# Attention stage of a two-model kernel: four units in flight, row and column halves of the array in turns, group outputs in one bank

## Reference

```python
R = H // G                                   # 16 heads, 4 groups of keys and values, 64 wide
sc = where(vis, einsum('bgrqd,bgnd->bgrqn', qb, k_cmp), NEG)         # 15 compressed blocks
p_cmp = softmax(sc) * any(vis)
o_cmp = einsum('bgrqn,bgnd->bgrqd', p_cmp, v_cmp)
sc = where(pos <= t, einsum('bgrqd,bgqkd->bgrqk', qb, ksel), NEG)    # selected blocks
o_slc = einsum('bgrqk,bgqkd->bgrqd', softmax(sc), vsel)
sc = where(wmask, einsum('bgrqd,bgkd->bgrqk', qb, kwin), NEG)        # window
o_win = einsum('bgrqk,bgkd->bgrqd', softmax(sc), vwin)
return gb[..., 0:1] * o_cmp + gb[..., 1:2] * o_slc + gb[..., 2:3] * o_win
```

## Time and profile before

| | us |
|---|---|
| median of three runs | 1864.11 |
| lowest and highest run | 1857.58, 1868.36 |
| the profiled execution | 1860.6 |
| its span in the trace | 1858.7 |
| PE busy, of the span | 1715.8 |
| DVE busy | 1038.0 |
| ACT busy | 791.7 |

### The profile page before, as it was taken

The page is one execution under the profiler, slowest core; times in us unless marked ns, Lnnn a source line. Parts: engine busy times, 40 slices in busy tenths (PEclk is TensorE's granted clock), DMA queues, the critical chain, the costliest instruction groups (busy, mean ns, idle before and its releaser), DMA issues.

```text
span 1858.7 us, 22342 instructions
## 1 busy us (share of the span) xinstructions
PE 1715.8 (92%) x8605; PEld 1414.5 (76%) x8605; DVE 1038.0 (56%) x1326; ACT 791.7 (43%) x963; POOL 96.7 (5%) x143
## 2 busy tenths in 40 slices
PE   6999978899999999989898989999899887789996
PEld 6788867688888788889855777888688673668885
DVE  4577654466655676645554435555548653655553
ACT  4434433365434444333455335555444433334441
POOL 1000000010000000010000003000100010200000
PEclk8999989999999999999899999999899895799998
DMA  8687734177864677633400425556365330536550
GB/s 288 201 277 262 233 108 157 40 255 252 268 226 147 229 259 262 225 104 101 167 33 1 139 69 174 190 189 213 108 231 204 109 106 1 170 125 203 181 181 23
DMA packets 210195, 311.74 MB, mean 168 GB/s; under 512 B 16537, under 2 KB 145589, under 8 KB 209872
## 3 DMA queue, kind: packets, MB, share of 16 engines
q1 hardware_dynamic: 204112, 288.90, 46.6%
q0 software_dynamic: 6016, 21.94, 3.4%
HBM read 306.59 MB, written 4.21 MB: 167 GB/s over the span
## 4 chain that ended last, share of the span: by engine, by line
PE 85%; DVE 6%; ACT 3%; issue 3%; DMA 1%; PEld 1%; POOL 1%; DVEq 0%; PEldq 0%; ACTq 0%; SPq 0%; POOLq 0%
PE ps L1994 24%; PE ps L1996 24%; PE ps L1995 24%; DVE wlo L1304 1%; PE ps L2035 1%; PE ps L2330 1%; PE ps L2116 1%; PE ps L2217 1%; PE ps L2315 1%; DMA area<-in_gate_b 1%; PE ps L2045 1%; PE ps L2198 1%; PE ps L2418 1%; PE ps L2306 1%; ACT xn L811 0%
## 5 line engine op out<-in xcount | busy, mean ns | idle before, releaser
L1304 DVE TENSOR_TENSOR wlo<-raw,whi 128x2048 fp32r<-128x2048 f32 x255 | 581.0, 2298 | 238.1 <-ACT whi L757 237.3
L757 ACT ACTIVATE whi<-raw 128x2048 fp32r<-128x2048 f32 x255 | 481.2, 1910 | 207.1 <-PE ps L1996 183.7
L1994 PE MATMUL ps<-wlo,aT_hi 128*128 128x512 f32 (+1 forms) x1280 | 500.2, 391 | 22.1 <-DVE aT_lo L1330 9.2
L1996 PE MATMUL ps<-whi,aT_hi 128*128 128x512 f32 (+1 forms) x1280 | 493.4, 385 | 0.0
L1995 PE MATMUL ps<-whi,aT_lo 128*128 128x512 f32 (+1 forms) x1280 | 493.0, 385 | 0.0
L1994 PEld LDWEIGHTS ps<-wlo,aT_hi 128*128 128x128 f32 x1280 | 244.1, 191 | 72.6 <-issue 15.0
L1996 PEld LDWEIGHTS ps<-whi,aT_hi 128*128 128x128 f32 x1280 | 243.5, 190 | 47.9
L1995 PEld LDWEIGHTS ps<-whi,aT_lo 128*128 128x128 f32 x1280 | 244.2, 191 | 45.1
L1994 PE MATMUL ps<-wlo,hT_hi 128*128 128x512 f32 x480 | 188.0, 392 | 5.4 <-DVE hT_lo L1421 3.0
L1996 PE MATMUL ps<-whi,hT_hi 128*128 128x512 f32 x480 | 187.6, 391 | 0.0
L1995 PE MATMUL ps<-whi,hT_lo 128*128 128x512 f32 x480 | 187.3, 390 | 0.0
(11 more groups left out here) (302 smaller groups left out, 1388.4 us busy)
## 6 DMA issues: line engine op xcount, KB each, us to landing
raw<-in_ffn_w_in SPq DMA_DIRECT2D x176, 512.0 KB, 4.9
raw<-in_ffn_w_out SPq DMA_DIRECT2D x88, 512.0 KB, 4.3
raw<-in_w_ff SPq DMA_DIRECT2D x64, 512.0 KB, 4.7
raw<-in_ada_w SPq DMA_DIRECT2D x48, 512.0 KB, 5.5
raw<-in_w_in SPq DMA_DIRECT2D x48, 512.0 KB, 4.7
raw<-in_xattn_w_kv SPq DMA_DIRECT2D x32, 512.0 KB, 7.0
raw<-in_xattn_w_q SPq DMA_DIRECT2D x16, 512.0 KB, 4.8
raw<-in_xattn_w_o SPq DMA_DIRECT2D x16, 512.0 KB, 4.9
```

The lines of the kernel that those rows point to most:

```text
L757: act.activation(to, of, ACT.Copy).then_inc(hi_ready[slot], 1)
L1304: dve.tensor_tensor(lo, of, hi, ALU.subtract).then_inc(lo_ready[slot], 1)
L1994: pe.matmul(o, lh, rl, start=start, stop=False, skip_group_check=True)
L1996: return pe.matmul(o, lh, rh, start=False, stop=stop, skip_group_check=True)
```

## The change

Nothing is computed that was not computed before, except one exponential of a single column. What moves:

- **Four in flight.** `Pb` gets a fourth buffer and scores a fourth bank (`u % 4`). `nmx`, `den` and `rec` become eight columns wide. What lay in the way moves to `spare`, an unused half of `gain`. DVE and ACT run `top(u + 3)` and `exps(u + 3)` behind `weigh(u)` and `keep(u)`.
- **Rows in turns.** `score_pair(p)` writes the scores of units `2p` and `2p + 1`, lower rows, upper rows, lower rows, upper rows. PE's loop goes over pairs: `score_pair(p + 2)`, `turn(2p)`, `turn(2p + 1)`, then `turn_cmp` or all of `values`.
- **Columns in turns.** `values(gi)` alternates between output partitions 0 to 63 and 64 to 127 term by term, and all groups use bank 7. So `values(gi)` waits for `out_lo(gi - 1)`, where it waited for `out_lo(gi - 2)`.
- **`out_lo` a unit later** in DVE's queue (`u % 4 == 2`).
- **The start.** `score_pair(0)` is issued ahead of the compressed scores, `top(0)` and `top(1)` ahead of the centring, `exps(0)` and `exps(1)` ahead of the compressed branch's exponential, and its weighing moves into the loop behind `weigh(1)` and `top(4)`. ACT issues an exponential of one column first, which loads its table. 20 matmuls of zeros stand ahead of the loop instead of 30; neither loop has any in it.

```diff
-        Pb = [xnf[:, 512 * b:512 * b + 512] for b in range(3)]
+        Pb = [xnf[:, 512 * b:512 * b + 512] for b in range(4)]
+        nmx4, den4, rec4 = small[:, 26:34], small[:, 34:42], small[:, 42:50]
+        spare = gain[:, 1, :]
...
+                    act.activation(small[:, 62:63], minus_half[:, 0:1], ACT.Exp)
+                    exps(0)
+                    exps(1)
                     act.wait_ge(cmp_centred, 1)
                     act.activation(cmpP, cmpP, ACT.Exp).then_inc(cmp_exped, 1)
-                    exps(0)
-                    exps(1)
+                    exps(2)
                     for u in range(32):
                         keep(u)
-                        if u + 2 < 32:
-                            exps(u + 2)
+                        if u + 3 < 32:
+                            exps(u + 3)
...
-                        if u >= 3:
-                            dve.wait_ge(probs_turned, U - 2)
+                        if u >= 4:
+                            dve.wait_ge(probs_turned, U - 3)
...
                     top(0)
                     top(1)
+                    centre_cmp()
+                    top(2)
                     for u in range(32):
                         weigh(u)
-                        if u + 2 < 32:
-                            top(u + 2)
-                        if u % 4 == 1 and u > 4:
+                        if u + 3 < 32:
+                            top(u + 3)
+                        if u == 1:
+                            weigh_cmp()
+                        if u % 4 == 2 and u > 4:
                             out_lo(u // 4 - 1)
...
+                    def score_pair(p):
+                        g, t, k = p // 4, p // 2 % 2, p % 2
+                        w = P * (t + 1)
+                        if p >= 2:
+                            pe.wait_ge(maxed, units.n + 2 * p - 2)
+                        for c, keys in ((0, ksT), (w, kwT)):
+                            for e in range(2):
+                                half = slice(64 * e, 64 * e + 64)
+                                last = pe.matmul(ps[:, (2 * p + e) % 4, c:c + w], qT[half, 2 * g + k, t * P:(t + 1) * P],
+                                                 keys[half, g, 0:w], start=True, stop=True)
+                                if c:
+                                    last.then_inc(scored, 1)
...
-                    def values(gi, half):
+                    def values(gi):
...
-                        if gi >= 2:
-                            pe.wait_ge(o_kept, groups.n + gi - 1)
+                        if gi:
+                            pe.wait_ge(o_kept, groups.n + gi)
+                        terms = [(vcmp[:, 64 * g:64 * g + 64], nsaPc[gi % 2][0:N_CMP])]
                         for j, v in enumerate((vs, vw)):
                             for m in range(t + 1):
                                 c = P * (j * (t + 1) + m)
+                                terms.append((v[:, m, 64 * g:64 * g + 64], nsaP[gi % 2][:, :, c:c + P]))
+                        for n, (v, probs) in enumerate(terms):
+                            for half in range(2):
+                                last = pe.matmul(ps[64 * half:64 * half + 64, 7, 0:256], v, probs[:, half::2, :],
+                                                 start=n == 0, stop=n == len(terms) - 1, skip_group_check=True)
+                        last.then_inc(pv_done, 1)
...
-                    score(0)
-                    score(1)
-                    keep_clock(30, 5)
-                    for u in range(32):
-                        if u + 2 < 32:
-                            score(u + 2)
-                        turn(u)
-                        if u % 4 == 2:
-                            turn_cmp(u // 4)
-                        if u % 4 < 2 and u >= 4:
-                            values(u // 4 - 1, u % 4)
-                    for half in range(2):
-                        values(7, half)
+                    score_pair(1)
+                    keep_clock(20, 4)
+                    for p in range(16):
+                        if p + 2 < 16:
+                            score_pair(p + 2)
+                        turn(2 * p)
+                        turn(2 * p + 1)
+                        if p % 2:
+                            turn_cmp(p // 2)
+                        elif p:
+                            values(p // 2 - 1)
+                    values(7)
```

More of the change, by code:

```diff
@@ L1023, in exps @@
                     def exps(u):
-                        U, t, b = units.n + u, u // 4 % 2, 2 * (u % 3)
+                        U, t, b = units.n + u, u // 4 % 2, 2 * (u % 4)
                         w = P * (t + 1)
@@ L1665, in nsa_attend @@
-                    every = [P, T, NSA_H, N_CMP]
[L1666 to L1671, removed]
@@ L1672, in nsa_attend, with centre_cmp @@
-                    dve.tensor_tensor(cmpP, cmpP, cmp_max.unsqueeze(3).to_broadcast(every), ALU.subtract).then_inc(cmp_centred, 1)
+                    def centre_cmp():
+                        mask = cst[:, C_CMP:C_CMP + 32].rearrange("p (t n) -> p t n", t=T)[:, :, 0:N_CMP]
+                        dve.wait_ge(cmp_scored, 2)
+                        for par in range(2):
+                            scores = ps[:, 6 + par, 0:256].rearrange("p (t h n) -> p t h n", t=T, h=NSA_H // 2)[:, :, :, 0:N_CMP]
+                            step(dve.tensor_tensor(cmpP[:, :, par::2, :], scores,
+                                                   mask.unsqueeze(2).to_broadcast([P, T, NSA_H // 2, N_CMP]), ALU.add))
+                        step(dve.tensor_reduce(cmp_max, cmpP, AX.X, ALU.max))
+                        dve.tensor_tensor(cmpP, cmpP, cmp_max.unsqueeze(3).to_broadcast(every), ALU.subtract)\
+                            .then_inc(cmp_centred, 1)
@@ new lines, in weigh_cmp @@
+                    def weigh_cmp():
+                        dve.wait_ge(cmp_exped, 1)
+                        step(dve.tensor_reduce(cmp_rec, cmpP, AX.X, ALU.add))
+                        step(dve.reciprocal(cmp_rec, cmp_rec))
+                        step(dve.tensor_tensor(cmp_rec, cmp_rec, gates[:, :, 0::3], ALU.mult))
+                        dve.tensor_tensor(cmpP, cmpP, cmp_rec.unsqueeze(3).to_broadcast(every), ALU.mult).then_inc(cmp_weighed, 1)
+                    every = [P, T, NSA_H, N_CMP]
@@ L2298, in nsa_attend @@
                     enter()
[L2300 to L2306, removed]
-                        pe.matmul(ps[:, u % 3, w:2 * w], q, kwT[half, g, 0:w], start=True, stop=True).then_inc(scored, 1)
+                    def score_pair(p):
[10 more added lines that the diff above has]
+                                    last.then_inc(scored, 1)
                     def turn(u):
@@ L2314, in turn @@
                         for m in range(2 * (t + 1)):
-                            last = pe.transpose(ps[:, 3 + u % 2, P * m:P * m + P], Pb[u % 3][:, P * m:P * m + P], ident)
+                            last = pe.transpose(ps[:, 4 + u % 2, P * m:P * m + P], Pb[u % 4][:, P * m:P * m + P], ident)
                         last.then_inc(probs_turned, 1)
-                    def values(gi, half):
+                    def values(gi):
                         g, t = gi // 2, gi % 2
@@ L2329, in values @@
                                 c = P * (j * (t + 1) + m)
-                                last = pe.matmul(o, v[:, m, 64 * g:64 * g + 64], nsaP[gi % 2][:, half::2, c:c + P],
-                                                 start=False, stop=j == 1 and m == t)
-                        if half == 1:
-                            last.then_inc(pv_done, 1)
+                                terms.append((v[:, m, 64 * g:64 * g + 64], nsaP[gi % 2][:, :, c:c + P]))
[4 more added lines that the diff above has]
+                        last.then_inc(pv_done, 1)
                     def turn_cmp(gi):
@@ L2340, in turn_cmp @@
                         for r in range(4):
-                            last = pe.transpose(ps[0:N_CMP, 5, P * r:P * r + P], cmpP[:, t, 4 * g + r, :], ident)
+                            last = pe.transpose(ps[0:N_CMP, 6, P * r:P * r + P], cmpP[:, t, 4 * g + r, :], ident)
                         last.then_inc(cmp_turned, 1)
+                    score_pair(0)
                     for t in range(T):
```

40 lines of the change are left out of this document (16 added, 24 removed).

## The result

| | before | after |
|---|---|---|
| median, us | 1863.88 (4 runs) | 1834.1 (4 runs, 1830.64 to 1836.34) |
| ratio | | 0.984, 95% interval 0.981 to 0.987 |
| span of the profiled execution | 1858.7 | 1830.7 |
| from the end of the matmuls ahead of the stage to its last `out_lo` | 108.4 | 78.1 |
| period of eight units | 21.90 | 14.07 |

What follows compares the result with a forecast made beforehand. PE was taken to bound the attention loop. After: 4 x 14.1 + 1.9 + 3.25 = 61.6 us, ending 31.7 earlier; less 6.0 for the clock, a 25.7 gain takes 1860.6 to 1834.9, range 1822 to 1850.

Steps and rivals of the forecast that it cites:

- What bounds the kernel, PE's blocks: Attention loop: PE bounds it; array halves overlap, so PE's work per period falls by 7.4 to 12.2 us.
- The next bound: Attention loop: ACT's 12.5 us per period is the floor, handovers come above; period 13.3 to 16.0, taken as 14.1.
- The fewer change-overs: PE's loop: fewer changes between block shapes, as a second turn follows a first; not counted, only on the good side.
- `values` waits for the group before: PE's queue stands behind out_lo of the group before; counted as nothing, 1.5 us per group if DVE were late.
- The start: Ahead of the loop: ten fewer zero matmuls at about 0.22 us each bring its start from 936.32 to 934.1.
- The stall behind the compressed weighing: Loop start: the compressed weighing stands ahead of weigh(2) in DVE's queue and PE waits for it, +1.9 us.
- The end and the sum: Loop end: last long values and outputs stand alone, 3.25 us; loop 61.6 us in all, from 934.1 to 995.7.
- The clock: Attention loop: two half-clock stretches of 6.8 us allowed, 2 x 3.0 = 6.0 us, cutting the gain to 25.7.
- 3.0 for 6.8: Inside the loop: one half-clock stretch of 6.8 us costs 3.0 us, from a period of 24.86 against 21.90.
- The rival that the clock stays at half: Attention loop: half clock makes periods 26.5 us, total 1878.5, slower; half clock through much of the loop, chance 0.10.
- It just moves forward: Stage behind attention: starts on weights long split, so it only shifts earlier with the loop's end, 31.7 us before clock.

Runs made afterwards that it cites:

- the pair unit by unit: Changed kernel with score_pair writing both scores of one unit, then both of the next, rows not in turns; median 1834.24 us, ratio 0.986.
- The extra copy: Changed kernel plus one more copy on ACT per group, as long as keep_cmp, into a place nobody reads; median 1833.59 us, ratio 0.987.
- the undone columns: Changed kernel with values doing all terms of output partitions 0 to 63 first, then 64 to 127, not in turns; median 1848.83 us, ratio 0.993.
- both moves together: Changed kernel with the compressed weighing ahead of top(4) and out_lo behind the fourth unit of the group; median 1828.93 us, ratio 0.984.
- the kernel with two units ahead: Changed kernel with DVE and ACT working two units ahead instead of three, PE's order kept; median 1840.2 us, ratio 0.9905.
- The kernel with buffers alone: Changed kernel with PE's earlier single scores and half-by-half values; four buffers, new start, one output bank kept; median 1859.09 us, ratio 0.9995.

## Why the prediction came out as it did

**What bounds the kernel, PE's blocks.** Right. Forecast for a long pair 1.06, measured 1.06. Long values of both halves 2.45 and 2.45. PE's work per period 12.2 and 12.2 to 12.3. L2377, L2501 and the order of L2306 and L2307 were the right rows for it. My reading of the earlier trace rows for rows was exact: adjacency is enough (1.07 us for the pair unit by unit).

**The next bound.** The number was right (14.1, measured 14.07), and the mechanism only in part. I took ACT's 12.5 as a floor and added 1.6 for handovers. ACT is busy for 11.9 with the same instructions, so 12.5 was no floor, and 2.1 us of idle are in the ring. (Records that follow each other at once overlap: `keep` from 972.56 lasts 0.57, and the next starts at 973.04. They follow each other at once more often now; that this is the whole difference wasn't tried.) The fewer change-overs that I left out did not show as less PE work. The extra copy and the undone columns show that work on ACT and on PE both lengthen the period in full, and the chain shows the ring through all three engines whose sum it is, not the busiest engine plus a gap. The Trainium skill's "TensorEngine Tiling (Array Packing)", section PSUM Bottleneck, says that copying out of PSUM may become the bound. The trace of the kernel with the extra copy agrees in that 0.48 us more of it per group costs 0.48, though ACT is not full (12.83 of 15.00 us).

**`values` waits for the group before.** Counted at nothing, and no such wait stands in the trace of the loop. Right.

**The start.** The loop's first score was forecast at 934.1 and came at 932.7. The zeros were priced right: 6.35 us, against 8.69 - 10 x 0.22 = 6.5. But they began at 926.38, not at 927.63, because the matmuls ahead of them ran faster. The compressed scores, in the chain before and after:

```profile
921.82 4.75 PE ps L2348 x64
```

```profile
922.36 3.48 PE ps L2367 x64
```

Before, the clock fell to half at 924.3, in the middle of them; after, at 927.1, under the zeros. The stall behind the compressed weighing is real: 1.88 us in DVE's queue, from 935.09 to 936.97, against 1.9. But not all of it was a loss, since DVE would have waited for `turn(0)` in part of it: with the weighing ahead of `top(4)`, `weigh(3)` ended 1.0 earlier.

**The end and the sum.** From the loop's first score to the last `out_lo` I had 61.6 without the clock and 67.6 with it. Measured: 996.86 - 932.73 = 64.1.

**The clock** is the term that was mis-sized: 6.0 for two stretches of 6.8 us. There were two in the loop, of 6.8 and 3.4 us. The sum leaves 64.1 - 61.6 = 2.5 for them, if the other terms are as forecast. The one at the end can be read by itself: the last long values took 3.26 instead of 1.95, and those of the compressed branch ahead of them 0.97 instead of 0.65, 1.6 us together. That leaves 0.9 for the stretch of 6.8. It fell where the loop fills: PE waited for `weigh(2)` and `weigh(3)` until 939.1 and was busy for only 5.75 of the 6.80 us. Inside the running loop the new kernels pay as before. With both moves together, one stretch of 3.4 us lengthened the period around it from 14.39 to 15.96, 1.6 us, where 3.0 for 6.8 gives 1.5. PE was busy for all of it:

```profile
952.50:956.00 3.50, 3.50 (x20) 2.19 (x21) 1.15 (x7) 1.23 (x6) 0.00 (x0) 0.51 0.00 0
```

In the kernel with two units ahead, one of 3.4 us lengthened a period from 16.35 to 17.69. So the 3.0 was a fair price inside the loop, and the term came out small because 3.4 us less stood at half and the longer stretch fell on the start. The rival that the clock stays at half did not come: whole periods ran at 1.00 though PE waits for 1.8 of 14.07 us. "TensorE: Matmul & The Clock Gate", Part 4 of the Trainium skill, made it likelier, as turns count for less. Turns and `turn_cmp` are 4.8 of PE's 12.3 us here, by the prices of the earlier trace rows, and the clock held.

**Behind the stage.** "It just moves forward" was too simple. The stage gave 30.3 us and the span fell by 28.0. From the stage's end to the last instruction it takes 831.3 us before and 833.9 after, with the same code. Busy time by stretch, first before, then after:

```profile
1528.50:1555.80 27.30, 17.29 (x44) 8.58 (x44) 10.08 (x43) 7.97 (x26) 0.00 (x0) 0.50 0.05 18
1555.80:1562.60 6.80, 4.01 (x19) 1.61 (x18) 1.43 (x5) 1.83 (x4) 0.00 (x0) 1.00 0.00 0
```

```profile
1500.60:1551.80 51.20, 39.50 (x106) 19.48 (x106) 15.92 (x73) 15.87 (x53) 0.00 (x0) 0.50 0.00 0
```

After, the second model's stage stays at half clock through what was a break of 6.8 us at full. I see no effect of the change in this. The kernel with buffers alone, whose stage ends where that of before does, takes 834.6 for this part, and among all the kernels it takes 830.1 to 836.4, in the changed one itself 833.9 and 836.3. The fourteen traces fall into two groups: six in which the half-clock stretch there is broken as before (830.1 to 832.4), among them four variants of the changed kernel, and eight in which it runs for 51.2 us (833.9 to 836.4). What decides between the two stays open.

So the profiled execution took 1832.8, forecast 1834.9. Loop start (-1.4) and clock (-3.5) came out better than thought, and 2.6 was lost behind the stage, which gives 1832.6: the total was nearer than its terms.

## What to carry to other kernels

Price a packed block from a neighbouring stage that issues the same form, and then ask two questions apart: how much work the packed engine keeps, and how long the ring of handovers is that goes through it. Here three engines were each busy for more than 80% of a period, and an instruction added on ACT or PE cost its full length; on DVE none was added. Where the chain shows such a ring, do not count an engine's idle time as slack. Before a filler of a waiting PE is removed, look whether it is on the chain at all; with the compressed weighing moved ahead it was not, and it kept the clock up.

## What was not expected

- Matmuls on the two row halves overlap when four records of one stand ahead of four of the other (1.07 us for a pair, as in turns), while ten records on one column half are not passed by the other's (4.90 us against 2.45). The two cases differ in more than the side.
- 0.96 us of ACT work per period lengthened it by 0.96 with ACT idle for 2.1.
- Without 20 matmuls of zeros that lay beside the chain, the granted clock stood at 0.50 for 23.9 us, and the stage took 2.3 us more.
- The same code behind the stage took 830.1 to 836.4 us, by where the half-clock stretches fell. The stage itself took 78.1 and 78.0 in two executions of the changed kernel, but 78.6 and 77.1 in two of the one with the weighing first. A change of a few us is better read in its stage than in the time, and there with the clock beside it.
- The price of a half-clock stretch hung on where it fell: about 0.9 us for 6.8 us while the loop filled, 1.6 for 3.4 us inside it.
